# Two heads' scores at a time in 64-row halves, low parts on GpSimd, and the mixer's later weight chunks in halves

## The reference, cut to what matters

```python
proj = h @ w_in[l]                       # h: (1, 272, 2048); q, k, v and u are columns of proj
q = _rmsnorm(q, q_norm_g[l]); k = _rmsnorm(k, k_norm_g[l])     # 16 heads of 64, 4 key/value heads
attn = _sliding_window_attention(q, k, v, attn_sinks[l])       # window 128, meta keys, sink, ALiBi
# S5 mixer: bu = u @ b_bar; states = scan(a, bu) over the sequence; y = real(states @ c) + d * u
g = jax.nn.gelu(y)
ssm = g * jax.nn.sigmoid(g @ w_glu + b_glu)
mix = jnp.concatenate([_rmsnorm(attn, attn_out_g[l]), _rmsnorm(ssm, ssm_out_g[l])], axis=-1)
h_res = h_res + mix @ w_out[l]
h_res = h_res + jnp.square(jax.nn.relu(_rmsnorm(h_res, norm_mlp_g[l]) @ w_up[l])) @ w_down[l]
```

## Time and profile before

| | us |
|---|---|
| median of 3 runs | 3089.47 (3088.95 to 3092.02) |
| the profiled execution's own time | 3089.37 |
| its span, from the first to the last instruction | 3087.6 |
| PE busy | 3066.5 (99%) |
| DVE busy | 1846.4 (60%) |
| ACT busy | 1453.3 (47%) |
| POOL busy | 718.9 (23%) |

### The profile page before, as it was taken

The page is one execution under the profiler, slowest core; times in us unless marked ns, Lnnn a source line. Parts: engine busy times, 40 slices in busy tenths (PEclk is TensorE's granted clock), DMA queues, the critical chain, the costliest instruction groups (busy, mean ns, idle before and its releaser), DMA issues.

```text
span 3087.6 us, 46008 instructions
## 1 busy us (share of the span) xinstructions
PE 3066.5 (99%) x16688; PEld 2623.5 (85%) x16688; DVE 1846.4 (60%) x2369; ACT 1453.3 (47%) x2250; POOL 718.9 (23%) x748
## 2 busy tenths in 40 slices
PE   8999999999999999999999999999999999999999
PEld 7888888888888888888888888888888888888887
DVE  5676655565555567675655555558786555555554
ACT  5454544444344545554343444452565434444343
POOL 1422232141411133041414141125130101001010
PEclk9999999999999999999999999999999999999999
DMA  6534555555656553455556555658534555555554
GB/s 243 191 142 168 191 211 201 203 203 183 218 186 220 202 191 137 164 193 204 203 183 218 189 218 191 225 214 304 189 110 164 191 191 191 191 191 190 191 191 163
DMA packets 70866, 598.06 MB, mean 194 GB/s; under 512 B 14448, under 2 KB 29040, under 8 KB 36672
## 3 DMA queue, kind: packets, MB, share of 16 engines
q1 hardware_dynamic: 59136, 588.17, 52.4%
q10 hardware_dynamic: 11184, 5.48, 0.6%
q0 software_dynamic: 400, 2.44, 0.2%
HBM read 577.92 MB, written 18.15 MB: 193 GB/s over the span
## 4 chain that ended last, share of the span: by engine, by line
PE 95%; DVE 2%; DMA 1%; ACT 1%; issue 0%; ACTq 0%; DVEq 0%
PE bank L680 94%; PE bank L792 1%; DVE w_lo L1732 1%; DMA yrow<-ys 1%; DMA urow<-us 0%; PE bank L951 0%; DMA u<-urow 0%; PE bank L840 0%; DMA par<-params 0%; DVE act_lo L2172 0%; DVE gbuf L2216 0%; DVE sb L2251 0%; PE bank L1118 0%; ACT act_hi L1568 0%; DVE ks L2194 0%
## 5 line engine op out<-in xcount | busy, mean ns | idle before, releaser
L680 PE MATMUL bank<-xg,w_hi 128*128 128x512 f32 (+1 forms) x4256 | 1431.4, 384 | 1.7 <-issue 1.3
L680 PE MATMUL bank<-xg,w_lo 128*128 128x256 f32 (+1 forms) x4064 | 1141.3, 281 | 0.0
L680 PEld LDWEIGHTS bank<-xg,w_hi 128*128 128x128 f32 x4256 | 787.0, 188 | 168.9 <-issue 2.0
L1726 DVE TENSOR_TENSOR w_lo<-raw,w_hi 128x1024 fp32r<-128x1024 f32 x512 | 673.6, 1352 | 426.9 <-ACT w_hi L1233 426.6
L1233 ACT ACTIVATE w_hi<-raw 128x1024 fp32r<-128x1024 f32 x512 | 514.1, 1052 | 634.5 <-PE bank L680 634.3
L680 PEld LDWEIGHTS bank<-xg,w_lo 128*128 128x128 f32 x4064 | 763.7, 188 | 0.9
L680 PE MATMUL bank<-w_hi,act_hi 128*128 128x512 f32 x1920 | 752.8, 392 | 2.0 <-issue 2.0
L680 PE MATMUL bank<-w_hi,act_lo 128*128 128x512 f32 x1920 | 747.7, 389 | 0.0
L680 PE MATMUL bank<-w_lo,act_hi 128*128 128x512 f32 x1920 | 747.3, 389 | 0.0
L1732 DVE TENSOR_TENSOR w_lo<-raw,w_hi 128x1024 fp32r<-128x1024 f32 x510 | 628.4, 1239 | 167.2 <-ACT w_hi L1222 166.6
L1222 ACT ACTIVATE w_hi<-raw 128x1024 fp32r<-128x1024 f32 x514 | 514.4, 1052 | 153.1 <-PE bank L680 123.1
(11 more groups left out here) (346 smaller groups left out, 1956.8 us busy)
## 6 DMA issues: line engine op xcount, KB each, us to landing
raw<-stream SPq DMA_DIRECT2D x260, 2048.0 KB, 7.7
stabs<-ssm_tabs SPq DMA_DIRECT2D x8, 920.0 KB
rdo<-stabs SPq DMA_DIRECT2D x8, 768.0 KB, 6.0
ssm_bc<-smat SPq DMA_DIRECT2D x8, 640.0 KB, 7.2
raw<-stream SPq DMA_DIRECT2D x4, 1024.0 KB, 8.4
stabs<-ssm_f SPq DMA_DIRECT2D x8, 512.0 KB
drv<-stabs SPq DMA_DIRECT2D x8, 512.0 KB, 7.2
trig<-stabs SPq DMA_DIRECT2D x8, 408.0 KB, 4.9
```

The source lines that it names most:

```text
L680: return pe.matmul(o, a, b, start=start, stop=stop, skip_group_check=True)
L1726: dve.tensor_tensor(flat_lo[j][:, 1024 * h:1024 * h + 1024], flat_raw[r][:, 2048 * j + 1024 * h:2048 * j + 1024 * h + 1024], flat_hi[j][:, ...
```

## The change

1. Chunks 3 to 7 of the second block are loaded in two halves of 1 MB, each of all 128 rows. The first half of chunk 3 is issued where the chunk was; every turn s = 3 to 11 of SP's loop ends with one half: chunk s // 2 + 2, half s % 2. Before the first tile of such a chunk ScalarE waits for both halves.
2. `scores2` makes the scores of two heads at once: each head's matmuls use only its own 64 rows of q2 and of the keys. It is called at the end of the odd slots. VectorE's wait for it counts pairs.
3. `gated_low` leaves VectorE's list. GpSimd does its work behind the bias of heads 1, 2, 4 and 6, with two instructions for a tile: a product with the gain, in place, and a difference.

```diff
-        CHUNKS_BEHIND = {4: 4, 6: 5, 8: 6, 10: 7}
+        HALF_CHUNKS = range(3, 8)
+        GATED_LOW = {1: 0, 2: 1, 4: 2, 6: 3}
...
+            def half_chunk(c, h):
+                if h == 0:
+                    sp.wait_ge(lo_ready, 4 * (R2 + c - 2) + 12)
+                sp.dma_start(raw[c % 2][:, 8 * h:8 * h + 8, :], stream[B2 + c][:, 2048 * h:2048 * h + 2048].rearrange("p (k n) -> p k n", n=CW))\
+                    .then_inc(landed[c % 2] if h else half_landed, 16)
             load_drive(2)
-            chunk(3)
+            half_chunk(3, 0)
             for s in range(3, 12):
...
-                if s in CHUNKS_BEHIND:
-                    chunk(CHUNKS_BEHIND[s])
+                half_chunk(s // 2 + 2, s % 2)
...
-            def scores2(h):
-                pe.wait_ge(sb2_ready, h - 1) if h >= 2 else pe.wait_ge(bu_out, T2)
-                g = h // 4
-                k = k2_own[:, g // 2, g % 2, :] if g % 2 == h % 2 else (k2_high if h % 2 else k2_low)[:, g // 2, :]
-                q = q2[:, h // 2, :]
-                mm(bank[4 + h % 2][:, 0:144], q[:, 0:128], k[:, 0:144], True, True)
-                mm(bank[4 + h % 2][:, 144:416], q[:, 128:256], k, True, True).then_inc(score2_done, 1)
+            def scores2(j):
+                pe.wait_ge(sb2_ready, 2 * j) if j else pe.wait_ge(bu_out, T2)
+                g = j // 2
+                keys = [(k2_own[:, g // 2, e, :] if g % 2 == e else (k2_low, k2_high)[e][:, g // 2, :])[SIDES[e], :] for e in range(2)]
+                for e in range(2):
+                    mm(bank[4 + e][:, 0:144], q2[SIDES[e], j, 0:128], keys[e][:, 0:144], True, True)
+                for e in range(2):
+                    last = mm(bank[4 + e][:, 144:416], q2[SIDES[e], j, 128:256], keys[e], True, True)
+                last.then_inc(score2_done, 1)
...
-                if 0 <= s < H2:
-                    scores2(s)
                 if 2 <= s < H2 + 2:
                     turn2(s - 2)
...
+                if s % 2 and s + 1 < H2:
+                    scores2((s + 1) // 2)
...
             def split_after(T):                       # ScalarE
                 c = (T + 2 - T_B2) // 2
+                if c in HALF_CHUNKS and T % 2 == 0:
+                    act.wait_ge(half_landed, 16 * (DEPTH + c - HALF_CHUNKS[0] + 1))
...
-                dve.wait_ge(score2_done, h + 1)
+                dve.wait_ge(score2_done, h // 2 + 1)
...
                 pool.tensor_copy(sb2[h % 2][:, SBW - 1:SBW], par_at("sinks", h)).then_inc(bias2_ready, 1)
+                if h in GATED_LOW:
+                    for n in gated_tiles(GATED_LOW[h]):
+                        done = 2 * GATED_LOW[h] + n // 2 % 2 + 1
+                        pool.wait_ge(shi_ready, done)
+                        pool.wait_ge(ssq_ready, done)
+                        pool.tensor_tensor(gbuf[:, n, :], gbuf[:, n, :], par_at("ssm2_g", n).to_broadcast([P, S]), ALU.mult).then_inc(gained_low, 1)
+                        pool.wait_ge(gained_low, done)
+                        pool.tensor_tensor(act_lo[:, n, :], gbuf[:, n, :], act_hi[:, n, :].bitcast(F32), ALU.subtract).then_inc(slo_ready, 1)
```

More of the change, by code:

```diff
@@ L474, in build @@
         slo_ready = sem("slo_ready")
+        gained_low = sem("gained_low")
         ahi_ready = sem("ahi_ready")
@@ L2219, in gate_times @@
                 dve.sem_inc(evac_done, 1)
[L2221 to L2225, removed]
             def heads_low(j):
@@ L2276, in _ @@
             biased2(2)
-            gated_low(0)
             gate_times(2)
@@ L2282, in _ @@
             normed2(3)
-            gated_low(1)
             gate_times(3)
@@ L2289, in _ @@
             biased2(5)
-            gated_low(2)
             heads_low(0)
@@ L2305, in _ @@
                     half_rooted(0)
-                if s == 6:
-                    gated_low(3)
             for c in range(NC):
```

## The result

| | before | after |
|---|---|---|
| median, us (6 runs each) | 3091.13 | 3102.93 |
| profiled execution's span, us | 3087.6 | 3100.8 |
| mean granted clock | 0.999 | 0.998 |

The ratio of after to before is 1.004, with a 95% interval of 1.0029 to 1.0051: the change made the kernel slower by 11.8 us. Forecast were 3100.5 us against 3089.47, 11.0 us more. The sum came out right, but not every term of it did, and part of the agreement is luck.

What follows compares the result with a forecast made beforehand. TensorE was taken as the bound, fed by a state chain without slack. Chunk halves +10.5, paired scores -4.1, new waits +4.3 and moved low parts +0.3 gave +11.0 us: 3100.5 us against 3089.47, range 3090.5 to 3106.

Steps and rivals of the forecast that it cites:

- What bounds it: Whole kernel: TensorE is 95% of the span; in the second block's mixer the state chain arrives just in time, without slack.
- Landing times: Mixer, loads of late second halves with tables: 1.43 MB in 6.2 us, 2.2 MB in 8.1 us, interpolated from two loads.
- Chunk 3's step: Mixer: late second half starts w_hi of tile 6 4.0 us late, making state(2) and read-out(2) 3.7 us late.
- the loop: Mixer: a late half makes a late state, which delays SP's next second half; grows 3.7 to 4 us a turn.
- the first term: Mixer, weight chunks 3 to 7 in halves: +10.5 us, bounds +6 and +14.
- Pairs: Attention stretch, scores of two heads at once: 0.90 us a pair, -4.1 us over eight, bounds -5.7 and +1.6.
- The rival without overlap: Attention stretch: paired scores do not overlap at all, attention +6.2 us with the mixer as forecast, 3106 us; chance 0.08.
- the rule that speaks against it: Attention stretch: changing tiling mode drains TensorE, some 0.2 us; paid by all eight pairs, saving 2.6 us, not 4.1.
- The new waits: Attention stretch: TensorE waits for sb 2.1 us at the third pair, 2.0 at the fourth, 0.2 at a turn; +4.3 us.
- Part 3: Attention stretch, low parts moved from VectorE to GpSimd: +0.3 us on the path, bounds -1.0 and +3.
- Paid once: Mixer: VectorE and GpSimd recover between chunks, only the first 4 us stand, attention adds 0.5; 3094 us, chance 0.13.
- the faster one: Mixer and attention: second halves land in time, u<-urow waits go, pairs save 4.1 us; 3082 us, chance 0.06.

Runs made afterwards that it cites:

- the kernel with the second half ahead: Kernel before with chunks 3 to 7 in halves, the second issued before SP's wait for the state and the table loads; 3089.56 us, ratio 0.9996.
- chunk 5 alone late: Kernel before with chunks 3 to 7 in halves issued together, except chunk 5's second half at the end of SP's next turn; 3094.51 us, ratio 1.001.
- part 1 alone: Kernel before with only the chunk halves of the change, second halves at the end of SP's turns; scores and low parts as before; 3101.79 us, ratio 1.0035.
- chunk 3 alone late: Kernel before with chunks 3 to 7 in halves issued together, except chunk 3's second half at the end of SP's next turn; 3103.32 us, ratio 1.004.
- four pairs: Kernel before with scores of two heads at once for heads 8 to 15 only; 3090.2 us, ratio 0.9996.
- two: Kernel before with scores of two heads at once only for heads 10 and 11 and heads 12 and 13; 3089.35 us, ratio 0.9998.
- 1.1 alone: Kernel before with only the low parts moved from VectorE to GpSimd; 3091.59 us, ratio 1.0; its attention stretch was 1.1 us longer.
- the pairs alone: Kernel before with only the scores of two heads made at once, whole chunks, low parts on VectorE; 3090.71 us, ratio 0.9997.

## Why the prediction was right, point by point

At full clock the change costs 8.5 us in the profiled executions (8.0 in the mixer, 0.7 in the attention stretch, and TensorE came to the mixer 0.2 us earlier), where 11.0 were forecast. The clock, which the forecast leaves out, took 4.7 us more than before. That 11.0 us forecast and 11.8 us in the median lie so close is thus partly luck; the direction and the place of the loss are not.

- **What bounds it.** Right. TensorE's waits and clock make up all but 0.8 us of the mixer's loss, and the state chain without slack is confirmed by the kernel with the second half ahead.
- **Landing times.** 1.43 MB were forecast to land at 2114.8 and 2.2 MB at 2139.1 and 2162.5; measured 2115.3, 2138.5 and 2162.2. The times agree, the terms do not. The second half of chunk 4 and the tables ahead of it took 10.8 us from SP's first load (2127.68 to 2138.47), not 8.1, but that load went out 3.2 us before the forecast's 2130.9, since state(2) was hardly late; the two errors cancel. For the chunks 3 and 5 it took 7.3 and 8.9 us, not 6.2 and 8.2. The interpolation was short each time, by 0.7 to 2.7 us; its lower point, the 4.0 us called alone, had chunk 3 issued 0.4 us behind it.
- **Chunk 3's step.** Too large by 3.1 us at the state: 0.6 us late, not 3.7, as GpSimd's turn gave 2.7 us back. That gain was named only as a lower bound (2.6 us), with 0.8 taken for all turns. So the loop, as forecast, starts a turn later: tile 8 is 6.9 us late because its second half waits for state(2) at all, hardly because that state is late, and only from there on does the lateness feed itself (state(4) 6.5 us late, tile 10 11.2 us; with chunk 5 alone late 5.1 us). In part 1 alone state(2) ended at 2129.61, 2.6 us late, with its last instruction at 1.75 us, and tile 8 still started at 2138.92, 0.4 us from the changed kernel's time.
- **What stands behind the waiting w_hi.** This step was missing. The forecast followed the wait on ScalarE into VectorE's w_lo and no further. In ScalarE's own list stand urow<-us and, for the next u, u<-urow. The chain after runs over them (12.7 us), and the waits for u<-urow, which were to vanish, stayed at 5.2 us. The run with chunk 3 alone late shows this mechanism by itself.
- **The clock.** Missing too: 3.1 us in the mixer, 1.7 in the attention stretch. At full clock the mixer lost 8.0 us and not 10.5; the clock made up the difference. So the first term was right by the sum of two errors, 2.5 too much and 3.1 too little.
- **Pairs.** 0.90 us forecast, 0.91 measured (2257.60 to 2258.51). Two heads' matmuls on the two halves of the rows start 10 ns apart:
```profile
2257.60 0.39 PE L688 MATMUL bank<-k_own,q 64*128 64x144 f32 x1
2257.61 0.39 PE L688 MATMUL bank<-k_high,q 64*128 64x144 f32 x1
...
2258.51 0.55 PE L1128 MATMUL bank<-tab,prob 128*128 128x128 f32 x3
```
  The Trainium skill, TensorE: Matmul & The Clock Gate, Part 3, says that matmuls smaller than the array, each at its own tile position, can run in it at the same time; the trace agrees. The rival without overlap is excluded. But the saving of 4.1 us was not reached: the stretch's matmul time fell by 3.0 us (93.5 to 90.5), by 1.2 with four pairs and by 0.6 with two, that is 0.3 to 0.4 us a pair and not 0.52. The rest is paid next to the pair. The last full-array matmul ahead of it takes 0.32 us to the pair's start, in place of 0.23 (after; before, up to the scores at 2275.59):
```profile
2288.99 0.39 PE L688 MATMUL bank<-w_hi,act_lo 128*128 128x512 f32 x1
2289.30 0.39 PE L688 MATMUL bank<-k_own,q 64*128 64x144 f32 x1
```
```profile
2275.36 0.39 PE L680 MATMUL bank<-w_hi,act_lo 128*128 128x512 f32 x1
```
  and the first step of the turn behind it takes 0.47 us in place of 0.42. That is 0.14 us a pair, 1.1 in all: most of what the rule that speaks against it was to add (1.5 us), so here that rule came nearer than the forecast.
- **The new waits.** At the third and the fourth pair and at the turn of head 3:
```profile
2267.33 0.39 PE L688 MATMUL bank<-k_low,q 64*128 64x144 f32 x1 [1.23 <-DVE sb L2257]
...
2271.57 0.90 PE L1128 MATMUL bank<-tab,prob 128*128 128x128 f32 x3 [1.69 <-DVE prob L2269]
...
2279.06 0.39 PE L688 MATMUL bank<-k_low,q 64*128 64x144 f32 x1 [2.30 <-DVE sb L2257]
```
  Forecast 2.1, 0.2 and 2.0 us, measured 1.2, 1.7 and 2.3: together 5.2 in place of 4.3. On the other side the wait at the first out half (1.96 us), which was to stay, is gone: it was only moved to those places. At full clock the stretch lost 0.7 us and 0.5 were forecast, but again by two errors that cancel: 3.0 us of matmul time saved and not 4.1, 3.6 us of waits added and not 4.6.
- **Part 3.** 0.3 us forecast; 1.1 alone, with instructions of 0.80 (product) and 1.01 us (difference) on GpSimd where 1 was taken. It is what makes the third pair wait.
- **The rivals.** "Paid once" is excluded by tile 10, 11.2 us late here and 5.1 with chunk 5 alone late, and the faster one by the half's landing, 7.0 us after its issue at 2108.30.

## What to carry to other kernels

When a wait is added to an engine, list everything behind it in that engine's own queue, the DMAs it issues before all, and look at which large transfer they now fall behind: here 7 us of delay at the issue made 14 us at the landing. Splitting a load is free, moving its second half behind a wait that depends on its own consumer is not. Work taken from the bounding engine pays only where it did not cover the evacuation or the bias that the next step needs; of 3.0 us of matmul time saved by the pairs alone, 0.5 were kept.

## What was not expected of the hardware

The scatter between executions of one kernel goes with the granted clock. Of 27 executions of the kernel before in one set, 7 at a mean clock of 0.998 took 3092.8 us on average, 18 at 0.999 took 3090.2, 2 at 1.0 took 3087.4. In the profiles a fall lasts some 3.4 us and takes up to 1.7 us, and falls come in different places in executions of nearly the same code, always behind waits of TensorE, of 1.5 to 3.6 us in all. With chunk 3 alone late there are two longer ones, of 6.8 and 10.2 us, around waits of some 8 us each; TensorE is busy for only 3.3 and 4.7 us of them, so they take 4.0 us together. Why one wait of 2 us brings a fall and another does not stays open. A wait of TensorE here costs its length and, in some executions, up to 1.7 us more.
